# Gated MLP of a transformer chain: two norms as one chain, LayerNorm a block ahead on VectorE, its turns by token tile

## The reference, cut to what matters

```python
x = x + 0.5 * swiglu(rms_norm(x, ffn2_norm), wg, wu, wd)    # D_FF = 2816
x = rms_norm(x, final_norm)                # the first block's end: this is the residual from here on
h = rms_norm(x, a_norm_g)                  # the second block's first norm, straight behind it
u, v, z = split(h @ w_in, 3)               # each 256 x 2048
u = gelu(u)
v = layer_norm(gelu(v), ln_g, ln_b)        # mean and variance over all 2048 columns of v
w_m = where(allowed, w_s, 0)               # 16 heads, 128 x 128: tokens of a group mixed
mixed = einsum('hts,bgshc->bgthc', w_m, v) + b_s
x = x + (u * mixed * silu(z)) @ w_out      # and then the shared K/V, chunk attention, a last norm
```

## Time and profile before

| | us |
|---|---|
| median of 3 runs (lowest, highest) | 940.37 (940.36, 940.55) |
| the profiled execution | 940.53 |
| its span, first to last instruction | 938.6 |
| TensorE matmuls busy | 890.8 (95% of the span) |
| VectorE / ScalarE / GpSimd busy | 569.0 / 477.5 / 83.2 |
| mean granted TensorE clock | 0.986 |

### The profile page before, as it was taken

How to read it: one execution, slowest core, us unless ns; L and a number is a source line. 1 busy time by engine, 2 the same in 40 slices (tenths; PEclk the granted TensorE clock), 3 DMA queues, 4 the chain that set the end, 5 groups by cost and what they waited for, 6 DMA issues and landing times.

```text
span 938.6 us, 14939 instructions
## 1 busy us (share of the span) xinstructions
PE 890.8 (95%) x6444; PEld 841.8 (90%) x6444; DVE 569.0 (61%) x599; ACT 477.5 (51%) x575; POOL 83.2 (9%) x86
## 2 busy tenths in 40 slices
PE   3999999999999999999999988989999988899996
PEld 3999999989999998999999977989999978899994
DVE  5688988876675556644444446445656557554554
ACT  5566676655553435434234344464555544563652
POOL 0022322200000000000000001012121110000000
PEclk9999999999999999999999997998999999999998
DMA  8955555555434554455555643745666645435401
GB/s 272 310 181 179 184 186 192 197 185 182 138 108 157 195 191 153 165 195 179 186 175 185 218 158 112 243 161 184 201 205 217 204 135 186 160 104 179 158 1 45
DMA packets 123906, 163.52 MB, mean 174 GB/s; under 512 B 3904, under 2 KB 110912, under 8 KB 123840
## 3 DMA queue, kind: packets, MB, share of 16 engines
q1 hardware_dynamic: 121584, 156.05, 50.7%
q0 software_dynamic: 1552, 6.29, 2.0%
q10 hardware_dynamic: 704, 0.21, 0.1%
HBM read 161.50 MB, written 1.05 MB: 173 GB/s over the span
## 4 chain that ended last, share of the span: by engine, by line
PE 88%; ACT 4%; DVE 4%; issue 2%; DMA 1%; POOL 1%; SPq 0%; DVEq 0%; POOLq 0%; ACTq 0%
PE pAcc L318 21%; PE pG L284 8%; PE pG L286 8%; PE pG L285 8%; PE pU L286 8%; PE pU L284 8%; PE pU L285 8%; PE pAcc L300 2%; PE pAcc L299 2%; PE pAcc L298 2%; PE pM L298 2%; PE pM L300 2%; PE pM L299 2%; ACT hi L248 1%; DMA raw<-in_ffn_wg 1%
## 5 line engine op out<-in xcount | busy, mean ns | idle before, releaser
L253 DVE TENSOR_TENSOR lo<-raw,hi 128x2048 fp32r<-128x2048 f32 x138 | 316.6, 2296 | 168.2 <-ACT hi L248 168.1
L248 ACT ACTIVATE hi<-raw 128x2048 fp32r<-128x2048 f32 x142 | 269.4, 1905 | 25.0 <-PE pAcc L318 10.8
L284 PE MATMUL pU<-xT_hi,hi 128*128 128x256 f32 x624 | 177.5, 284 | 0.0
L285 PE MATMUL pU<-xT_lo,hi 128*128 128x256 f32 x624 | 176.7, 283 | 0.0
L286 PE MATMUL pU<-xT_hi,lo 128*128 128x256 f32 x624 | 176.7, 283 | 0.0
L284 PE MATMUL pG<-xT_hi,hi 128*128 128x256 f32 x560 | 160.7, 287 | 4.4 <-DVE xT_lo L748 3.5
L285 PE MATMUL pG<-xT_lo,hi 128*128 128x256 f32 x560 | 160.2, 286 | 0.0
L286 PE MATMUL pG<-xT_hi,lo 128*128 128x256 f32 x560 | 160.2, 286 | 0.0
L284 PEld LDWEIGHTS pU<-xT_hi,hi 128*128 128x128 f32 x624 | 119.8, 192 | 0.0
L285 PEld LDWEIGHTS pU<-xT_lo,hi 128*128 128x128 f32 x624 | 119.8, 192 | 0.0
L286 PEld LDWEIGHTS pU<-xT_hi,lo 128*128 128x128 f32 x624 | 119.8, 192 | 0.0
(11 more groups left out here) (275 smaller groups left out, 1500.9 us busy)
## 6 DMA issues: line engine op xcount, KB each, us to landing
raw<-in_a_w_in SPq DMA_DIRECT2D x24, 1024.0 KB, 5.3
raw<-in_ffn_wg SPq DMA_DIRECT2D x22, 1024.0 KB, 5.4
raw<-in_ffn_wu SPq DMA_DIRECT2D x22, 1024.0 KB, 5.4
raw<-in_ffn_wd SPq DMA_DIRECT2D x22, 1024.0 KB, 5.0
raw<-in_w_in SPq DMA_DIRECT2D x16, 1024.0 KB, 5.4
raw<-in_a_w_out SPq DMA_DIRECT2D x8, 1024.0 KB, 4.9
raw<-in_w_kv SPq DMA_DIRECT2D x8, 1024.0 KB, 5.4
raw<-in_b_w_qz SPq DMA_DIRECT2D x8, 1024.0 KB, 5.6
```

The source lines that it names most:

```text
L248: act.activation(HI[n % NHL][:, :], RAW[n % NRAW][:, :], ACT.Copy).then_inc(S["hi"], 1)
L253: dve.tensor_tensor(LO[n % NHL][:, :], RAW[n % NRAW][:, :], HI[n % NHL][:, :].bitcast(f32), ALU.subtract).then_inc(S["lo"], 1)
L284: pe.matmul(o, wk, xh, start=(k == 0), stop=False)
L285: pe.matmul(o, wk, xl, start=False, stop=False)
```

## The change

1. **Turn ffn2→gated MLP** by token tile, in new functions `act_pair` and `dve_pair`. With r1 the first norm's factor and g its gain, the second norm's mean square is r1²·mean((x·g)²), so both factors come from sums over X and over X·g (`a_xg`): v1 = mean(x²) + eps, v2 = mean((x·g)²) + eps·v1, and GpSimd takes both to the power −1/2 in one operation (`("pair", t)`). XN gets (x·g)·v2^−1/2·gain4 at once; the first norm itself (X·v1^−1/2·g) is written later, behind the turn. Each half row now has one more VectorE product and its square is of X or of X·g.
2. **TensorE's order** there: tile 0 is transposed inside `contract_last`; the first three v blocks do tile 0 first, then tile 1.
3. **v statistics** on VectorE: BN_STATS of each 256 columns right behind their gelu, BN_AGGR at the end; ScalarE's two long squares go.
4. **LayerNorm on VectorE, a block ahead** (`v_ln`): (v − mean)·gain, then ·rstd + bias, four SCALAR_TENSOR_TENSOR into one of two buffers; GpSimd's two operations a block go, it only issues DMAs.
5. **First mixing later**: `mix(0)` stands behind the z block of iteration 1. W_s's copies (`w_s`) come before the lo part of the second next block.
6. **The product** gelu(u)·silu(z) is made while the mixing runs; behind the mixing stand b_s (one operation instead of two) and one product instead of two.
7. **Turn gated MLP→chunk attention** by `dve_turn` and `act_turn`.
8. `bias_out` moves behind the last iteration's hi parts in ffn1; `warm` activations of one element load ScalarE's tables early (one for Sigmoid in the mixer, 15 in the gated MLP). The gain of norm 4 is loaded in ffn2's second iteration instead of at the turn.

The same 6444 matmuls are issued. The core of the diff:

```diff
-UNITS = [(0, 0), (0, 1), (1, 0), (1, 1), (2, 0), (2, 1), (3, 0), (4, 0), (3, 1), (4, 1),
+UNITS = [(0, 0), (0, 1), (1, 0), (1, 1), (2, 0), (2, 1), (4, 0), (4, 1), (3, 0), (3, 1),
...
         def pe_gmlp(pe):
-            transposes(pe, 3, 0)
             n = NTH["vgate", "v", 0]
-            pe.wait_ge(S["lo"], n + 1)
...
+            for c in range(3):
+                pe.wait_ge(S["lo"], n + c + 1)
+                if c == 0:
+                    pe.wait_ge(S["xt_lo"], 12 + 1)
+                    to_tokens(pe, n, ACC[0], XT, (0,), half_way=12 + 2)
+                elif c == 1:
+                    to_tokens(pe, n + 1, ACC[1], XT, (0,))
+                else:
+                    pe.wait_ge(S["res"], 12)
+                    to_tokens(pe, n + 2, ACC[2], XT, (0,), ks=range(0, 4))
+                    transposes(pe, 3, 1)
+                    to_tokens(pe, n + 2, ACC[2], XT, (0,), ks=range(4, KD))
             pe.wait_ge(S["xt_lo"], 12 + 3)
-            to_tokens(pe, n, ACC[0], XT, (1,), half_way=12 + 4).then_inc(S["used"], 1)
-            for c in range(1, 8):
-                n = NTH["vgate", "v", c]
-                pe.wait_ge(S["lo"], n + 1)
+            for c in range(3):
+                to_tokens(pe, n + c, ACC[c], XT, (1,), half_way=0 if c else 12 + 4).then_inc(S["used"], 1)
+            for c in range(3, 8):
+                pe.wait_ge(S["lo"], n + c + 1)
                 if c >= 4:
                     pe.wait_ge(S["a_v"], 2 * (c - 4 + 1))
-                to_tokens(pe, n, ACC[c % 4], XT, (1,) if c == 1 else (0, 1)).then_inc(S["used"], 1)
-            for i in range(8):
...
+            for i in range(8):
+                n = NTH["gmlp", "z", i]
+                pe.wait_ge(S["lo"], n + 1)
+                pe.wait_ge(S["silu"], H0["gmlp"] + i)
+                to_features(pe, n, G, XT).then_inc(S["used"], 1)
+                if i == 1:
+                    mix(0)
+                w_s_transposed(i)
+                pe.wait_ge(S["lo"], n + 2)
+                pe.wait_ge(S["act_b"], ACT_B0["gmlp"] + i)
+                to_features(pe, n + 1, U, XT).then_inc(S["used"], 1)
+                if i:
+                    mix(i)
                 if 0 < i < 7:
                     contract(pe, "gmlp", i - 1)
-            contract_last(pe, "gmlp")
+            contract_last(pe, "gmlp", 4)
...
-                if bias and i == NF - 2:
-                    bias_out(act)
+            if ph == "ffn1":
+                bias_out(act)
...
+            warm(act, 0, ACT.Sigmoid)
...
+        def act_pair(act, n):
+            hi(act, n + 1)
+            def square_to(m, src, k):
+                if m > 1:
+                    act.wait_ge(S["ssq"], 12 + m - 1)
+                act.activation((SA, SB)[m % 2][:, :], src, ACT.Square, scale=D ** -0.5,
+                               accum_out=ST[:, k:k + 1]).then_inc(S["ssq"], 1)
+            def square_x(m, t, c):
                 act.wait_ge(S["res"], 8 + 2 * t + c + 1)
-                square(act, 3, t, c)
...
+                square_to(m, X[:, half_row(t, c)], 12 + 2 * t + c)
+            def square_xg(m, t, c):
+                act.wait_ge(S["a_xg"], 2 * t + c + 1)
+                square_to(m, XN[:, half_row(t, c)], 16 + 2 * t + c)
+            for c in range(2):
+                square_x(2 * c, 0, c)
+                square_xg(2 * c + 1, 0, c)
+            hi(act, n + 2)
+            xt_hi(act, 3, XT, 0)
+            xt_hi(act, 3, XT, 1)
+            square_x(4, 1, 0)
+            hi(act, n + 3)
+            square_x(5, 1, 1)
+            square_xg(6, 1, 0)
+            square_xg(7, 1, 1)
             xt_hi(act, 3, XT, 2)
             xt_hi(act, 3, XT, 3)
+        def act_gmlp(act):
             for c in range(8):
                 n = NTH["vgate", "v", c]
                 act.wait_ge(S["used"], n + 1)
...
+        def dve_pair(dve, n):
+            def times_gain(t, c):
+                dve.wait_ge(S["res"], 8 + 2 * t + c + 1)
+                dve.wait_ge(S["gain1"], 16 * 2)
+                dve.tensor_tensor(XN[:, half_row(t, c)], X[:, half_row(t, c)], GAIN[1][:, c * 512:(c + 1) * 512],
+                                  ALU.mult).then_inc(S["a_xg"], 1)
+            def variances(t):
+                v1, v2 = ST[:, 38 + 2 * t:39 + 2 * t], ST[:, 39 + 2 * t:40 + 2 * t]
+                x0, x1, g0, g1 = (ST[:, k + 2 * t:k + 2 * t + 1] for k in (12, 13, 16, 17))
+                dve.wait_ge(S["ssq"], 12 + 4 * t + 3)
+                dve.tensor_scalar(v1, x0, x1, 1e-6, ALU.add, ALU.add).then_inc(S["a_pair"], 1)
+                dve.wait_ge(S["a_pair"], 2 * t + 1)
+                dve.tensor_scalar(v2, v1, 1e-6, g0, ALU.mult, ALU.add).then_inc(S["a_pair"], 1)
+                dve.wait_ge(S["a_pair"], 2 * t + 2)
+                dve.wait_ge(S["ssq"], 12 + 4 * t + 4)
+                dve.tensor_scalar(v2, v2, g1, None, ALU.add).then_inc(S["var"], 1)
+            def both_norms(t):
+                dve.wait_ge(S["rsqrt"], RS_ORDER.index(("pair", t)) + 1)
+                dve.wait_ge(S["gain0"], 16 * 3)
+                for c in range(2):
+                    o = XN[:, half_row(t, c)]
+                    dve.scalar_tensor_tensor(out=o, in0=o, scalar=ST[:, 39 + 2 * t:40 + 2 * t],
+                                             in1=GAIN[0][:, c * 512:(c + 1) * 512], op0=ALU.mult,
+                                             op1=ALU.mult).then_inc(S["xn"], 1)
+            lo_half(dve, n + 1, 0)
+            for c in range(2):
+                dve.wait_ge(S["acc_end"], 6 + c + 1)
+                add_acc(dve, 0, c, 0.5)
+                times_gain(0, c)
+            lo_half(dve, n + 1, 1)
+            variances(0)
+            both_norms(0)
+            lo_half(dve, n + 2, 0)
+            dve.wait_ge(S["acc_end"], 6 + 3)
+            add_acc(dve, 1, 0, 0.5)
             xt_lo(dve, 3, XT, 0)
             xt_lo(dve, 3, XT, 1)
-            rows(dve, 3, 1, X)
-            lo(dve, n - 2 + LEAD)
-            variance(dve, 4, 1)
-            rows(dve, 4, 1, XN)
+            dve.wait_ge(S["used"], NTH["ffn2", "down", NF - 1] + 1)
+            add_acc(dve, 1, 1, 0.5)
+            times_gain(1, 0)
+            times_gain(1, 1)
+            lo_half(dve, n + 2, 1)
+            variances(1)
+            both_norms(1)
+            lo_half(dve, n + 3, 0)
             xt_lo(dve, 3, XT, 2)
             xt_lo(dve, 3, XT, 3)
-            lo(dve, n - 1 + LEAD)
...
+            lo_half(dve, n + 3, 1)
+            for t in range(NT):
+                for c in range(2):
+                    o = X[:, half_row(t, c)]
+                    dve.scalar_tensor_tensor(out=o, in0=o, scalar=ST[:, 38 + 2 * t:39 + 2 * t],
+                                             in1=GAIN[1][:, c * 512:(c + 1) * 512], op0=ALU.mult,
+                                             op1=ALU.mult).then_inc(S["xn"], 1)
...
+            def v_ln(i):
+                if i > 1:
+                    dve.wait_ge(S["a_mix"], i - 1)
+                dve.wait_ge(S[f"a_par{i % 2}"], 16 * (i // 2 + 1))
+                par, x = APAR[i % 2], VL[i % 2]
+                for t in range(NT):
+                    dve.scalar_tensor_tensor(out=x[:, t * BC:(t + 1) * BC], in0=v3(VG[:, :], NT)[:, t, i * BC:(i + 1) * BC],
+                                             scalar=ST[:, 70 + t:71 + t], in1=par[:, 0:BC], op0=ALU.add,
+                                             op1=ALU.mult).then_inc(S["a_vg"], 1)
+                if i == 0:
+                    dve.wait_ge(S["rsqrt"], RS_ORDER.index(("ln",)) + 1)
+                for t in range(NT):
+                    dve.wait_ge(S["a_vg"], 2 * i + t + 1)
+                    o = x[:, t * BC:(t + 1) * BC]
+                    dve.scalar_tensor_tensor(out=o, in0=o, scalar=ST[:, 72 + t:73 + t], in1=par[:, BC:2 * BC],
+                                             op0=ALU.mult, op1=ALU.add).then_inc(S["a_vs"], 1)
...
+            def gated(i):
+                dve.wait_ge(S["silu"], H0["gmlp"] + i + 1)
+                dve.wait_ge(S["act_b"], ACT_B0["gmlp"] + i + 1)
+                dve.tensor_tensor(SB[:, :], SB[:, :], SA[:, :], ALU.mult).then_inc(S["a_ss"], 1)
                 dve.wait_ge(S["a_mix"], i + 1)
-                dve.wait_ge(S["a_par"], 16 * (i + 1))
                 m4, x4 = (v[:, :].rearrange("p (h g t) -> p h g t", h=2, g=NT) for v in (M, MX))
-                for g in range(NT):
...
+            v_ln(0)
+            lo(dve, n + 11)
+            w_s(0)
+            n = NTH["gmlp", "z", 0]
+            lo(dve, n + 4)
+            v_ln(1)
+            lo(dve, n + 5)
+            gated(0)
+            h_lo(dve, "gmlp", 0)
+            w_s(1)
+            lo(dve, n + 6)
+            for i in range(1, 8):
+                n = NTH["gmlp", "z", i]
+                gated(i)
+                if i < 7:
+                    v_ln(i + 1)
+                    lo(dve, n + 5)
                     h_lo(dve, "gmlp", i)
-                if i < 7:
-                    lo(dve, n + 1 + LEAD)
-                if 0 < i < 7:
```

(44 more changed lines are left out.)

159 lines of the change are left out of this document (57 added, 102 removed).

## The result

The changed kernel takes 918.66 us (median of 4 runs, 918.22 to 919.65), the kernel before 940.46 in the same comparison (940.36 to 941.54): ratio 0.9767, 95% interval 0.9750 to 0.9784. The prediction was 918.0 (914.5 to 925). The profiled execution took 918.86 us, its span 917.0, 21.6 less than before.

The account below looks back on a forecast made before the run. TensorE, 95% busy, bounds the kernel, so only its waits and slow clock can go. Gains 2.2 + 0.9 + 9.4 + 6.3 + 0.4 + 3.7 = 22.9 us take 940.5 to 917.6, with 0.4 for signals 918.0; range 914.5 to 925.

Parts of the forecast that it names:

- End of ffn1 and the table: End of ffn1: wait on the last h_lo goes, gain 2.2 us; Sigmoid's table loaded earlier, gain 0.9 us.
- Turn ffn2→gated MLP: Turn between these stages: loss falls from 11.5 to 2.1 us at full clock, gain 9.4 us (bounds 5.5 and 11.5).
- v statistics: v blocks: BN_STATS, taken as 0.4 us each, hides in VectorE's 3.5 us idle per block; no gain or loss.
- First mixing: Gated MLP: v ready about 624.5 against a mixing at 637 instead of 631; wait and half clock go, gain 6.3 us.
- Last iteration: End of the gated MLP: one product behind the mixing goes, gain 0.4 of TensorE's 1.1 us wait.
- Turn to chunk attention: Gated MLP to chunk attention: timed from gates→ffn2, 25.8 us shortened, gain 3.7 us, still bound by VectorE.
- The rival on the clock: The clock falls in a new turn behind short waits: one turn 921 us, both 924; chance 0.20.
- the 0.4 for signals: Whole kernel: 0.4 us added for signals not counted, taking 917.6 to 918.0 us.
- a granted clock of 0.5 behind either turn: Sign at the turns to gated MLP and chunk attention: clock 0.5 behind either would make the prediction wrong.
- The other signs: ffn1's 2.2 and gates' 0.9 us waits gone, pair's rows at 8.2, v-to-contraction 25 to 26, chunk turn 22 us.
- the rival "slower": Gated MLP's iterations: VectorE's order makes the mixing late, TensorE waits in each; 952 us with 10 us longer chain; chance 0.03.
- the chain as long as two: Turn ffn2→gated MLP: VectorE and ScalarE alternate, transposes 5 us late as before, 3.9 us more, 921.9 us; chance 0.12.

Follow-up runs that it names:

- u_bias: Changed kernel with ffn1's bias sum again copied to ScalarE's side two iterations before the end, not behind the last hi part; 920.68 us.
- u_sigmoid: Changed kernel without the early operation that loads ScalarE's table for Sigmoid; 920.19 us (918.67 to 921.91).
- two_chains: Changed kernel, turn ffn2→gated MLP still by token tile, but its two norms one behind the other again, with a second variance and power; 922.05 us.
- t0_behind: Changed kernel with tile 0's transposes in the turn ffn2→gated MLP behind the whole contraction, not ahead of its last quarter; 918.96 us.
- late_only: Kernel before with only the first mixing moved behind the following z block; 945.05 us against 940.82, ratio 1.0046.
- rows_first: Changed kernel, in the turn to chunk attention the K/V norm's partner's four rows ahead of a half and a whole lo part on VectorE; 915.96 us.
- mix_early: Changed kernel with only the first mixing back ahead of the u block of iteration 0; 919.11 us.
- no_warm_gmlp: Changed kernel without the 15 operations in the gated MLP that load ScalarE's tables early; 919.05 us.
- pair_better: Changed kernel, in the turn ffn2→gated MLP tile 0's variance ahead of a half lo part on VectorE, the next half behind xt_lo; 918.05 us.
- silu_first: Changed kernel, in the first iteration of chunk attention the silu of z ahead of a hi part on ScalarE; 915.71 us.
- best: Changed kernel with the orders of rows_first, pair_better and silu_first together; 913.42 us, ratio to the kernel before 0.9706.
- power_alone: best with the turn ffn2→gated MLP's second half lo part behind both norms' product, so VectorE idles during GpSimd's power; 912.10 us.

## Why the prediction was right

**Method.** Its sum was made from waits and slow stretches that end inside a stage, and no stage took back what another gave up to the end of the gated MLP. The term of every stage that was changed is within 0.3 us. That the total came within 0.9 us of the profiled execution is in part luck: a loss of 1.55 us that the sum did not have stands against 0.7 us of gain that it did not have either.

**End of ffn1 and the table.** Right, each 0.25 too low: a wait's bracket counts from the end of the matmul before it, which the next one would have overlapped by 0.16 (0.39 long, 0.23 apart), and the first matmul behind the wait takes 0.47 instead of 0.39. u_bias and u_sigmoid show the same 0.25.

**Turn ffn2→gated MLP.** Right in size and mechanism: rows at +7.9 (predicted +8.2), xT_lo's wait 0.38 (0.55), tile 1 without a wait, clock 1.00. The first wait is 0.95 instead of 1.35: the variance starts at +5.6 instead of +5.8, and the next VectorE operation behind the power stands 0.82 later, not 0.9.

The part of the joint chain is borne out by an experiment (two_chains). For the order by token tile the match of these times is all there is, and of that order the place of tile 0's transposes inside the contraction is worth nothing (t0_behind).

**v statistics.** The 0.4 taken for one BN_STATS holds: it takes 0.43 (600.76), two stand between two lo parts, and the v blocks have no wait.

**First mixing.** The 6.3 came as 6.12, but the text gives two reasons where one works. It set v at 624.5 against "a mixing at 637 instead of 631"; v is in time for either. late_only shows that the later place alone does harm.

**Last iteration.** 0.25 instead of 0.4: the wait is 0.82, was 1.08.

**Turn to chunk attention.** Tile 0 transposed at +6.9, tile 1 at +12.6 after a wait of 0.47 (predicted 0.6), xTk_lo at +14.3, the lo parts' end at +18.8, the end of the last transposes at +22.2 (22.1): the measure taken from gates→ffn2 carried over to 0.1 us, except the wait for xTk_lo, 1.08 instead of 1.5. That it "stays bound by VectorE" and would be 3 us less without the lo parts: rows_first moved them and got 2.4. No run puts the old turn back, so its 3.5 us rests on these times, not on an experiment.

**What it missed.** The rival on the clock (0.20) looked at the new turns. In the changed kernel's trace it fell there at no cost or not at all; it fell behind an old wait that nobody had touched, for 1.55 us. The changed stages add up to 22.9 us as predicted; the start of the program came 0.2 earlier and the 0.4 for signals was not needed, which makes 0.6 to 0.7 of the 1.55, and the other 0.9 lies between 918.0 and the profiled 918.86. But the rival was nearer than this trace shows: the changed turns lost 1.46 us to the clock in u_sigmoid, behind a wait of 1.5, and some 1.5 us in two_chains, behind one of 2.5.

By its own sign, "a granted clock of 0.5 behind either turn", the prediction would have failed: in the turn to chunk attention the clock is at 0.50 from 758.7 to 762.2. The sign was too strict. Slow matmuls cost nothing while TensorE would otherwise wait for rows; what tells is when the next block starts. The other signs came as written. In the iterations of the gated MLP there is no wait, so the rival "slower" falls, and the pair's first wait of 0.95 rules out the chain as long as two.

## What to carry to other kernels

When a wait is removed, ask of the waits that stay what they cost besides their length: the 1.9 us wait was worth 3.35 where the clock fell behind it and would be worth 1.8 where it did not. In the turn with two norms the split by token tile seems to be worth more (6.4 us, by subtraction) than joining the norms (3.1, by experiment). The order on the engine that carries the chain is worth a second look: a few moves of lo parts and one of a hi part brought 6 us more (5.2 between the medians), over a quarter of what the whole rebuild did. A small GpSimd operation on the critical path wants VectorE idle while it runs, or busy with copies out of PSUM, not with an operation that has both inputs in SBUF.

## What the runs showed of the hardware

**The clock falls behind the same wait in some traces and not in others.** From the silu at this wait to the next iteration's it takes 32.20 us where the clock stays at 1.00 (before, late_only, u_bias) and 33.75 where it falls to 0.50, the lower of the two levels (the changed kernel, u_sigmoid, two_chains, t0_behind, mix_early, no_warm_gmlp, pair_better, rows_first 33.79). TensorE waits 1.91 us in all of them; ahead of it stand large matmuls at full rate and 12 transposes, in u_bias and the changed kernel the same ones. Between u_bias and the changed kernel two things differ, and neither sorts the traces. The changed kernel has the slow stretch at 758.7, but t0_behind has none and its clock fell too. The wait comes 3.0 us later in u_bias, but it ends at 792.39 there, where the clock stayed, and at 792.51 in two_chains, where it fell. What decides is left open. Without the wait (silu_first, best, power_alone) the interval is 32.2 in all three.

**GpSimd is slowed by VectorE.** The two-column power takes 0.70 us with VectorE idle (554.26, 553.28) and 1.61 with a half lo part beside it (553.82); LayerNorm's operation 1.29 and 3.19. By the Trainium skill, page "SBUF — State Buffer", section "Who interferes with whom", a VectorE instruction with two SBUF inputs contends with a GpSimd instruction that reads SBUF, because its second input comes through the read interface that the two share, and whoever issues first keeps the other out. The runs agree: the power's extra 0.91 us is most of the 1.05 that the half lo part (553.65 to 554.87) still had to go. In the other order it is VectorE that loses: at 645.69 in the kernel before GpSimd's operation came first and took 1.29, and the lo part begun beside it at 646.36 took 2.76 instead of 2.29. Copies out of PSUM did neither: GpSimd's operation at 661.77 took 1.29 with two of them (0.42 and 0.29 us) beside it.
